# Weights loaded in pairs of chunks, with a changed head and tail, in a hybrid decoder trunk

## The reference

```python
h = x
# layer 0: Mamba-2 mixer. w_in is 2048 x 10304, a causal conv of width 4, silu, softplus of dt,
# a state-space scan in chunks of 128, gate, RMS norm by group, w_out is 4096 x 2048
# layer 1: grouped-query attention in a window of 128 with sinks, on one shared K/V (kv_w, w_q, w_o)
h = _layernorm(DEEPNORM_ALPHA * h + mix, ln_g[layer, 0], ln_b[layer, 0])
h = _layernorm(DEEPNORM_ALPHA * h + _sqrelu_mlp(h, mlp_w1[layer], mlp_w2[layer]), ln_g[layer, 1], ln_b[layer, 1])
# _sqrelu_mlp: jnp.square(jax.nn.relu(h @ w1)) @ w2, w1 is 2048 x 8192, w2 is 8192 x 2048
# _layernorm: (x - mean) * rsqrt(var + 1e-5) * g + b over the 2048 features
```

## Time and profile before

| what | value |
|---|---|
| median of 3 runs | 2373.24 us (2373.2 to 2373.24) |
| profiled execution, device time | 2373.24 us |
| its span, first to last instruction | 2371.4 us |
| mean granted TensorE clock | 0.998 |
| PE matmul busy | 2359.3 us, 99% |
| DVE busy | 1572.0 us, 66% |
| ACT busy | 1167.4 us, 49% |
| weight loads | 818 of 512 KB, median 4.1 us from issue to landing |

### The profile page before, as it was taken

One profiled execution on the slowest core, in us unless ns is written; L12 is line 12 of the kernel. 1 busy time (PEld: TensorE's weight loads), 2 busy tenths in 40 slices (PEclk: granted clock), 3 DMA queues, 4 the chain that ended last, 5 costly groups with the idle time before them and its releaser, 6 DMA issues.

```text
span 2371.4 us, 32219 instructions
## 1 busy us (share of the span) xinstructions
PE 2359.3 (99%) x12564; PEld 1995.1 (84%) x12564; DVE 1572.0 (66%) x2116; ACT 1167.4 (49%) x1741; POOL 55.2 (2%) x97
## 2 busy tenths in 40 slices
PE   9999999999999999999999999999999999999998
PEld 8888888888888888888888888778888888888886
DVE  8888888876577556456456576766864654655655
ACT  5555555564354444344344354774543443443441
POOL 3000000000000000000000000000000000000000
PEclk9999999999999999999999999999999999999999
DMA  7655556556656655655655646336565565565563
GB/s 257 226 196 196 193 188 195 191 189 222 192 197 233 204 187 188 197 185 194 196 187 192 195 154 202 126 126 208 201 231 187 191 199 186 190 195 187 192 195 108
DMA packets 122874, 455.14 MB, mean 192 GB/s; under 512 B 13664, under 2 KB 13792, under 8 KB 120432
## 3 DMA queue, kind: packets, MB, share of 16 engines
q1 hardware_dynamic: 119952, 433.83, 56.4%
q0 software_dynamic: 2784, 19.47, 2.2%
HBM read 450.55 MB, written 2.16 MB: 191 GB/s over the span
## 4 chain that ended last, share of the span: by engine, by line
PE 99%; DVE 0%; DMA 0%; ACT 0%; SPq 0%; DVEq 0%; issue 0%
PE ps L410 26%; PE ps L435 17%; PE ps L436 16%; PE ps L437 16%; PE ps L416 13%; PE ps L468 2%; PE ps L466 2%; PE ps L467 2%; PE ps L487 1%; PE ps L538 1%; PE ps L652 1%; PE ps L679 1%; PE ps L667 0%; PE ps L546 0%; DMA xin<-in_x_by_channel 0%; PE ps L387 0%
## 5 line engine op out<-in xcount | busy, mean ns | idle before, releaser
L1183 DVE TENSOR_TENSOR wlo<-raw,whi 128x1024 fp32r<-128x1024 f32 x818 | 996.2, 1224 | 668.0 <-ACT whi L758 662.7
L758 ACT ACTIVATE whi<-raw 128x1024 fp32r<-128x1024 f32 x814 | 856.4, 1057 | 841.2 <-PE ps L437 479.0
L410 PE MATMUL ps<-actA,whi 128*128 128x512 f32 x2672 | 639.3, 391 | 0.0
L410 PEld LDWEIGHTS ps<-actA,whi 128*128 128x128 f32 x2672 | 491.6, 188 | 96.3
L435 PE MATMUL ps<-whi,actB 128*128 128x512 f32 x1056 | 412.8, 391 | 0.0
L436 PE MATMUL ps<-wlo,actB 128*128 128x512 f32 x1056 | 411.0, 389 | 0.0
L437 PE MATMUL ps<-whi,actB 128*128 128x512 f32 x1056 | 410.9, 389 | 0.0
L416 PEld LDWEIGHTS ps<-actA,wlo 128*128 128x128 f32 x2672 | 342.8, 191 | 13.2
L416 PE MATMUL ps<-actA,wlo 128*128 128x256 f32 x2672 | 346.9, 283 | 0.0
L435 PEld LDWEIGHTS ps<-whi,actB 128*128 128x128 f32 x1056 | 198.3, 188 | 42.9 <-issue 1.3
L437 PEld LDWEIGHTS ps<-whi,actB 128*128 128x128 f32 x1056 | 198.3, 188 | 41.3
(11 more groups left out here) (193 smaller groups left out, 1703.1 us busy)
## 6 DMA issues: line engine op xcount, KB each, us to landing
raw<-in_chunks SPq DMA_DIRECT2D x818, 512.0 KB, 4.1
csb<-cs_rows POOLq DMA_DIRECT2D x8, 1024.0 KB, 6.0
gb<-in_ln_g POOLq DMA_DIRECT2D x4, 1024.0 KB, 6.7
gb<-in_ln_b POOLq DMA_DIRECT2D x4, 1024.0 KB, 9.5
xin<-in_x_by_channel SPq DMA_DIRECT2D x4, 512.0 KB, 7.1
res<-in_x POOLq DMA_DIRECT2D x2, 1024.0 KB, 8.6
out<-res SPq DMA_DIRECT2D x8, 256.0 KB, 2.7
kz<-kz POOLq DMA_DIRECT2D x2, 256.0 KB, 7.0
```

Of the source, the lines that this page charges most:

```text
L410: e.matmul(ps[:, b, :], whi[:, s, k * P:(k + 1) * P], act[:, kt, :, :].rearrange("p a n -> p (a n)"), start=(kt == 0), stop=False)
L758: e.activation(whi[:, s, :], raw[:, r, :], ACT.Copy).then_inc(w_hi_done, C.up(w_hi_done))
L1183: e.tensor_tensor(wlo[:, s, :], raw[:, r, :], whi[:, s, :].bitcast(F32), ALU.subtract).then_inc(w_split, C.up(w_split))
```

## The change

Three edits go together. First, from chunk 22 on one load brings chunks k and k + 1, 1 MB, into two neighbouring slots of `raw`; it waits until both slots are free, that is until chunk k - 3 is split. ACT waits for a landing only at even chunks. Second, in the head x is split in halves of each quarter (`x_half_split` tells of the first half), there are 13 instead of 17 zero products, and in the first SSM group ACT makes the first term of each convolution (`conv_first`, signalled by `conv_begun`) where DVE had a TENSOR_SCALAR (L1273). Third, in the last norm of the second half of the tokens, DVE multiplies the blocks 0 and 1 by the gain before PE has finished; PE then adds them, through the identity, and minus the mean times the gain, through a diagonal matrix, into PSUM banks 6 and 7. DVE centres only blocks 2 and 3, and these are stored first.

```diff
@@ -54,6 +54,7 @@
 RAW = 4
 RING = 8
 LEAD = 6
+FIRST_CHUNKS = 22
 GROUP_CHUNKS = 20
 SLAB_CHUNKS = 32
 
...
@@ -74,7 +75,8 @@
 assert sum(FILLS_OF_UNIT) == len(FILLS)
 
 
-OUTPUT_PIECES = [(h, slice(c, c + BLK)) for h in range(NH) for c in range(0, D, BLK)]
+LAST_BLOCKS = [slice(c, c + BLK) for c in range(0, D, BLK)]
+OUTPUT_PIECES = [(h, cols) for h in range(NH) for cols in (LAST_BLOCKS[2:] + LAST_BLOCKS[:2] if h else LAST_BLOCKS)]
 
 
 class Counts:
...
@@ -318,10 +326,19 @@
                     loaded[s], C.up(loaded[s]))
                 n[0] += 1
 
+            def load_pair(k):
+                if C.any(w_split, back=-1):
+                    e.wait_ge(w_split, C.now(w_split, back=-1))
+                C.n[w_split] += 2
+                s = n[0] % RAW
+                e.dma_start(raw[:, s:s + 2, :], t["chunks"][bass.ds(k, 2)].rearrange("a p n -> p a n")).then_inc(
+                    loaded[s], C.up(loaded[s]))
+                n[0] += 2
+
             def load_group(g):
 
-                for k in range(GROUP_CHUNKS):
-                    load(2 + g * GROUP_CHUNKS + k, also_next=(k == 11), wait=(k != 12))
+                for k in range(0, GROUP_CHUNKS, 2):
+                    load_pair(FIRST_CHUNKS + (g - 1) * GROUP_CHUNKS + k)
 
             def load_x(g):
                 e.dma_start(xin[:, 4 * g:4 * g + 4, :], t["x_by_channel"][g].rearrange("p (k n) -> p k n", k=4)).then_inc(
...
@@ -348,8 +365,8 @@
             with C.loop(3, before, 2) as i:
                 for b in range(2):
                     load_group(2 * i + 2 + b)
-            for k in range(2 + NG * GROUP_CHUNKS, TOTAL):
-                load(k)
+            for k in range(2 + NG * GROUP_CHUNKS, TOTAL, 2):
+                load_pair(k)
             for h, cols in OUTPUT_PIECES:
                 e.wait_ge(output_ready, C.next(output_ready))
                 e.dma_start(out[0, h * P:(h + 1) * P, cols], res[:, h, cols]).then_inc(out_done, C.up(out_done))
...
@@ -378,10 +395,11 @@
                 fill(0)
                 fill(1)
                 for q in range(4):
-                    e.wait_ge(act_split, C.next(act_split))
+                    e.wait_ge(x_half_split, C.next(x_half_split))
                     e.wait_ge(first_hi_done, C.next(first_hi_done))
                     for k in range(4):
                         if k == 2:
+                            e.wait_ge(act_split, C.next(act_split))
                             e.wait_ge(w_hi_done, C.next(w_hi_done))
                         for b in range(2):
                             e.matmul(ps[:, b, :], whi[:, q, (2 * k + b) * P:(2 * k + b + 1) * P],
...
@@ -493,7 +511,7 @@
                     e.matmul(ps[:, 1, 0:P], st[:, 0:P], st[:, 0:P], start=True, stop=True)
 
             e.wait_ge(zeros_ready, C.next(zeros_ready))
-            zero_products(17)
+            zero_products(13)
 
             def dt_transposes():
                 e.wait_ge(dt_summed, C.next(dt_summed))
...
@@ -742,6 +760,17 @@
             column_block_by_halves(2, actB, after=((), during(0)))
             mlp({7: lambda: None})
 
+            def last_norm():
+                for i in range(2):
+                    e.wait_ge(gained, C.next(gained))
+                    e.matmul(ps[:, 6 + i, :], ident[:, :], res[:, 1, LAST_BLOCKS[i]], start=True, stop=False)
+                e.wait_ge(diag_ready, C.next(diag_ready))
+                for i in range(2):
+                    e.matmul(ps[:, 6 + i, :], minus_mean_diag[:, :], gb[:, 0, LAST_BLOCKS[i]], start=False, stop=True).then_inc(
+                        shifted, C.up(shifted))
+
+            last_norm()
+
 
 
         @block.scalar
...
@@ -754,7 +783,8 @@
                 i = C.n[w_hi_done]
                 if i < TOTAL:
                     s, r = i % RING, i % RAW
-                    e.wait_ge(loaded[r], C.next(loaded[r]))
+                    if i < FIRST_CHUNKS or i % 2 == 0:
+                        e.wait_ge(loaded[r], C.next(loaded[r]))
                     e.activation(whi[:, s, :], raw[:, r, :], ACT.Copy).then_inc(w_hi_done, C.up(w_hi_done))
 
             def step():
...
@@ -777,7 +807,8 @@
 
             def x_hi(g):
                 e.wait_ge(x_in[g], C.next(x_in[g]))
-                hi(actA[:, 4 * g:4 * g + 4, 0, :], xin[:, 4 * g:4 * g + 4, :])
+                for k in (4 * g, 4 * g + 2):
+                    hi(actA[:, k:k + 2, 0, :], xin[:, k:k + 2, :])
 
             def split_in_halves(k):
                 e.wait_ge(loaded[k], C.next(loaded[k]))
...
@@ -829,6 +860,13 @@
                 products()
                 e.activation(mcross[:, i % 2, :], ps[:, 4 + i % 2, T:2 * T], ACT.Copy).then_inc(
                     cross_out, C.up(cross_out))
+
+            def conv_first(i):
+                x = i % 2
+                e.wait_ge(free[x], C.next(free[x]))
+                e.activation(xh[:, x, :], xpad[:, x, 3:3 + T], ACT.Identity,
+                             scale=cwg[:, 0, i * 5 + 3:i * 5 + 4], bias=cwg[:, 0, i * 5 + 4:i * 5 + 5]).then_inc(
+                                 conv_begun, C.up(conv_begun))
 
             def tanh(i):
                 e.wait_ge(conv_done, C.next(conv_done))
...
@@ -875,6 +913,8 @@
                 split_weights()
                 cross(2, 4)
                 cross(3, 4)
+                conv_first(2)
+                conv_first(3)
                 step()
                 tanh(2)
                 step()
...
@@ -1204,7 +1248,8 @@
                 return x[:, bass.ds(g * GH, GH)].unsqueeze(2).broadcast_to([P, GH, HD])
 
             def x_lo(g):
-                lo(actA[:, 4 * g:4 * g + 4, 1, :], xin[:, 4 * g:4 * g + 4, :], actA[:, 4 * g:4 * g + 4, 0, :])
+                for k, done in ((4 * g, x_half_split), (4 * g + 2, act_split)):
+                    lo(actA[:, k:k + 2, 1, :], xin[:, k:k + 2, :], actA[:, k:k + 2, 0, :], done)
 
             e.memset(st[:, 0:P], 0.0).then_inc(zeros_ready, C.up(zeros_ready))
             e.memset(xpad[:, :, 0:3], 0.0)
...
@@ -1263,16 +1308,18 @@
                 e.tensor_tensor(xpad[:, x, 3:3 + T], ps[:, x, 0:T], xpad[:, x, 3:3 + T], ALU.add).then_inc(
                     free[x], C.up(free[x]))
 
-            def conv(i, par, summed=False):
+            def conv(i, par, begun=False):
 
                 x = i % 2
                 w = [cwg[:, par, i * 5 + k:i * 5 + k + 1] for k in range(5)]
-                if not summed:
+                if begun:
+                    e.wait_ge(conv_begun, C.next(conv_begun))
+                else:
                     conv_sum(i)
-                e.wait_ge(free[x], C.now(free[x]))
-                e.tensor_scalar(xh[:, x, :], xpad[:, x, 3:3 + T], w[3], w[4], ALU.mult, ALU.add).then_inc(
-                    dve_step, C.up(dve_step))
-                e.wait_ge(dve_step, C.now(dve_step))
+                    e.wait_ge(free[x], C.now(free[x]))
+                    e.tensor_scalar(xh[:, x, :], xpad[:, x, 3:3 + T], w[3], w[4], ALU.mult, ALU.add).then_inc(
+                        dve_step, C.up(dve_step))
+                    e.wait_ge(dve_step, C.now(dve_step))
                 for k in (2, 1):
                     e.scalar_tensor_tensor(xh[:, x, :], xpad[:, x, k:k + T], w[k], xh[:, x, :], ALU.mult, ALU.add).then_inc(
                         dve_step, C.up(dve_step))
...
@@ -1597,17 +1648,28 @@
 
                 slab_end = C.now(w_used, back=-7)
                 e.wait_ge(gains_in, C.next(gains_in, 2))
-                for h in range(NH):
-                    half_statistics(h, slab_end)
-                    pieces = [cols for hh, cols in OUTPUT_PIECES if hh == h]
-                    for cols in pieces:
+                def centred_pieces(h, blocks):
+                    for cols in blocks:
                         e.scalar_tensor_tensor(res[:, h, cols], res[:, h, cols], mvb[:, h, 0:1], gb[:, 0, cols],
                                                ALU.subtract, ALU.mult).then_inc(centred, C.up(centred))
                     e.wait_ge(rstd_ready, C.next(rstd_ready))
                     e.wait_ge(centred, C.now(centred))
-                    for cols in pieces:
+                    for cols in blocks:
                         e.scalar_tensor_tensor(res[:, h, cols], res[:, h, cols], rstd[:, h:h + 1], gb[:, 1, cols],
                                                ALU.mult, ALU.add).then_inc(output_ready, C.up(output_ready))
+
+                half_statistics(0, slab_end)
+                centred_pieces(0, LAST_BLOCKS)
+                for cols in LAST_BLOCKS[:2]:
+                    e.tensor_tensor(res[:, 1, cols], res[:, 1, cols], gb[:, 0, cols], ALU.mult).then_inc(gained, C.up(gained))
+                half_statistics(1, slab_end)
+                e.tensor_scalar(minus_mean_diag[:, :], ident[:, :], mvb[:, 1, 0:1], -1.0, ALU.mult, ALU.mult).then_inc(
+                    diag_ready, C.up(diag_ready))
+                centred_pieces(1, LAST_BLOCKS[2:])
+                for i, cols in enumerate(LAST_BLOCKS[:2]):
```

(33 more changed lines are left out.)

## The result

The changed kernel takes 2393.0 us in the median of 4 runs (2390.23 to 2393.47), the kernel before 2373.23 in the same session (4 runs, 2373.2 to 2373.24). The ratio is 1.0082, with an interval of 1.007 to 1.0094. The forecast was 2375.5 with a range of 2371.3 to 2380.0: the sign of the pairs was right, their size was not. The profiled execution took 2393.47, its span is 2391.7; 20.3 us more than before.

A forecast was written before the change was run, and what follows sets the result against it. The prediction took PE to bound the kernel, busy 2359.3 of 2371.4 us. From 2373.24, head -0.4, tail -1.1, norms +0.4, +0.2 and +0.2, MLP openings +3.0 summed to +2.3: 2375.5 us, range 2371.3 to 2380.

The forecast's parts named there:

- the sign of the pairs: Paired loads cost time: 0.4 and twice 0.2 us at the norms, 3.0 at the two MLP openings.
- the one on the landing: A 1 MB pair lands 4.6 us after issue, between 4.3 and about 5.0, hidden in steady stretches with 6.4 left.
- Elsewhere I take nothing: Outside the norms and MLP openings, SSM groups included, pairs cost 0; the convolution banks' room is gone at landings of some 5.5.
- my own rule: At an MLP opening two landings stand in the chain, so 0.1 us more in a landing costs 0.2.
- my wait of 1.5: At each MLP opening PE waits 1.25 us for a bank, plus 0.25 because DVE comes late from the norm.
- The norms: PE waits for the centred block after late pairs: 0.4 us at the first norm, 0.2 at each of two others.
- none between 100 and 600: Sign to look for in the changed trace: no PE idle time between 100 and 600 us.
- Rival 2: Landings of 5.0 and more at openings and first groups, early groups some 1.5 us: 2379.8; past 2385 at 5.5; chance 0.20.
- the later release: In the paired loads, chunk k leaves when k - 3 is split, not k - 4, and lands with chunk k + 1.
- The head: At the kernel's start, earlier first products and x split in halves gain 0.4 us, bounds 0 and 0.75.
- The terms on ACT: First SSM group, six convolution terms moved from DVE to ACT: nothing, or up to 0.4 us against the head's gain.
- The tail: After PE's end, two centrings fewer (1.38 us) less 0.26 for the diagonal matrix: gain 1.1, bounds 0.7 and 1.4.

The follow-up runs named there:

- second trace of the changed kernel: The changed kernel run again as it is, with nothing edited, on the chip of other follow-up runs: 2391.65 us, ratio 1.0081 to the kernel before.
- ends only: The changed kernel with single loads in place of the paired ones, so the head and tail edits alone: 2371.73 us, ratio 0.9996 to the kernel before.
- two singles: The changed kernel with each pair issued as two 512 KB transfers at the pair's moment, ACT waiting for each: 2373.23 us, ratio 1.0004 to the kernel before.
- wait for both: As two singles, but ACT waits for both landings before it copies the first chunk: 2386.52 us, ratio 1.0058 to the kernel before.
- pairs only: The kernel before with the paired loads alone, old head and tail: 2387.21 us, ratio 1.0056 to the kernel before.

## Why the prediction was wrong

**The step that failed is the one on the landing** ("How long does 1 MB take? ... I take 4.6"), with the two things built on it: a sum that used one landing for every place, and "Elsewhere I take nothing". Landings were 4.8 where it is quiet, but 6.0 to 7.6 at the four places that cost most.

- *The quiet landing.* All pairs, then those of 860 to 1400 us, in the changed kernel:

```profile
DMA to landing us min/median/max: 4.7/4.8/9.7
...
DMA to landing us min/median/max: 4.7/4.8/6.4
```

  0.2 more than I took, 0.4 per opening by my own rule. That is the small part. (The Trainium skill, DMA: Bandwidth & Descriptors, Anatomy of one DMA, has a fit for POOL's path from which 4.4 is the estimate for 1 MB. `csb`, also 1 MB and on that path, takes 5.0 in the median here: the measurements decide, and both lie above.)
- *The landing at the openings.* It is read from the two pairs issued in 700 to 712 us, and from three near 1691:

```profile
DMA to landing us min/median/max: 7.6/7.7/7.8
...
DMA to landing us min/median/max: 5.2/6.0/6.2
```

  Two pairs are in flight together there, 702.33 and 704.60, where I had counted one. That alone does not make them late: the two issued at 1641.8 and 1644.3 in the same trace landed in

```profile
DMA to landing us min/median/max: 4.8/4.8/4.8
```

  What else differs is told in the last section. 3.0 us more in the first landing makes my wait of 1.5 into 4.5; PE waited 4.09 and 0.41 just before. The mechanism (two landings in the chain, `mcross` and the addition behind chunk 242) was right in every link. How large it comes out is a draw: in the second trace of the changed kernel the first pair lands in 5.1, PE waits 2.36, and the opening costs 4.2 instead of 7.3.
- *The slow clock behind a wait*, a term that my sum did not have: 2.3 at the first opening, 1.5 at the second, about 1.6 at the third norm. By the page, PE is busy for 2370.5 us, in the kernel with the ends only for 2362.7 with the same 12564 products: 7.8 of the 21.4 us between these two spans are products that ran slower, 13.6 are idle time.
- *The norms.* First: 0.4 forecast, 0.9 measured, by the order that I gave. Second, at 1402 us: 0.2 forecast, 0.6 measured. Third: 0.2 forecast, 4.2 measured. The order is the same at all three, so the "little more room" was not there, but what sets the third apart is again its landing. The chains of the second and of the third norm have, in front of the copy, split, addition and centring:

```profile
1390.69 4.72 DMA raw<-in_chunks
...
1661.19 6.67 DMA raw<-in_chunks
```

  PE's block comes 0.59 late at the second. 1.95 more of landing makes 2.54, and 2.51 was measured. PE waited 2.36 for the centred block and ran on at a granted clock of 0.73 until 1680:

```profile
1674.19 1.92 DVE L1599 TENSOR_SCALAR res<-res,small 128x512 f32<-128x512 f32 x4 [0.44 <-POOL small L1922]
1674.79 1.11 PE L505 MATMUL ps<-ident,res 128*128 128x128 f32 x4 [2.36 <-DVE res L1599]
```

- *"Elsewhere I take nothing."* The early groups cost 3.8: 1.5 at 83 us, where a convolution bank comes late because the pair 28/29 lands in 6.7 to 8.6 us (over four traces) beside POOL's 1 MB `csb`, 1.2 at the banks of 89 and 98 us, with landings of 4.8 to 5.2, and 1.1 at 160 and 166 us, where a pair lands in 7.1 beside the next `csb`. The last place contradicts "none between 100 and 600". Rival 2 named the early groups, with this cause, at 1.5. But it too knew one landing for all and no slow clock: its 4.9 as the bound was never reached in the quiet stretches, and "every group would lose some tenths", its way past 2385, did not happen. Attention cost 0.9, for which the forecast had nothing.
- *What a pair costs apart from its length.* I counted the later release. The runs put it at 1.5 (two singles, within their scatter), the wait of the first chunk for the whole megabyte at 13.3, and the one transfer in place of two at 5 to 6.5 (2391.65 and 2393.0 against 2386.52; all eight runs of the changed kernel lie above all four of "wait for both", while why one transfer is worse than two was not tried). The prediction held the second inside the landing's length and never priced it by itself: a single chunk lands after 3.1 at the least and can be copied while the next is in flight.
- *The head*: 0.4 forecast, 0.67 measured in this trace, and 0.15 to 0.70 in the ten traces with the new head, so 0.4 was about right, and which value a run has is a draw (the old head of "pairs only" comes out 0.15 ahead too). The ninth product started at 9.70, not 9.90, and its releaser is ACT's copy of the weights, not x. The terms on ACT, taken as nothing, move the tightest split from 25.59 to 24.80. The 26 zero products end at 6.39, not 6.0; the first product still starts at 6.15.
- *The tail*: DVE's part 1.14 against 1.12, exact. The last step in the trace is only -0.7 to -0.8, because the end comes 0.4 later behind DVE in this run. With the ends only the whole tail gives 1.1.

## What to carry to other kernels

Before two loads are joined, ask who can start on the first half: the join takes from the consumer the time by which the second half lands later, and in a chain through several loads it takes it each time. Size the landing at the place where the chain is tight, by the slow landings of the trace too and not by the quiet median alone (the earlier trace rows had 10.5 as its longest); a steady stretch with slack says nothing about it. And price a wait of PE with the slower products that can follow it: behind waits of 2.18 to 4.09 us they were 50 to 70% of the wait on top here, behind one of 2.90 nothing.

## What the runs showed of the hardware

In this trace a late pair waits for the last of its parts. The transfers from 702 to 713 us: busy tenths of the DMA engines and GB/s in 40 slices, and the queues.

```profile
DMA  0002190379999999998989999982000000000000
GB/s 0 0 0 60 45 164 0 119 298 372 402 387 447 372 387 402 387 343 298 268 253 357 447 402 372 432 343 104 30 30 30 15 30 30 30 30 0 0 0 0
...
q8 instruction: 1, 0.02, 0.5%
```

From 709.7 to 711.9 us only 15 to 30 GB/s move, what one of the 16 engines carries of some 430: the second pair waits for one late engine. One packet that fetches instructions, 0.5% of 16 engines in 11 us or 0.9 us of one, lies in this window, as in that of 1690 to 1701 and in that of the third norm's pair (1661 to 1668, where the pair's last 1.5 us move 23 GB/s). The window of the two pairs that landed in 4.8 (1641 to 1650) has no such packet of 16 KB. Of the 26 pairs that took more than 6 us in the changed kernel's trace, nine had a transfer of POOL in flight, and at the other 17 such a packet lies within the flight or up to 2 us ahead of it. Yet most pairs with one land in about 4.9. That the fetch is what makes the engine late was not tried. The Trainium skill, DMA: Bandwidth & Descriptors (Two DMAs through the same engine are not ordered), says that data has landed only with the full increment of the semaphore, and that nothing orders the 16 engines among each other; this trace agrees. My reading, not tested by itself, is that with a larger transfer more of the data hangs on the last engine.

The clock did not fall after every wait: behind 2.90 us in "wait for both" sixteen products took 3.96 (granted clock 1.00), behind 2.18 in the changed kernel seven took 3.35 instead of 1.87. The length of the wait alone does not decide it; what else does, these runs don't show.
